# A three-block transformer kernel in float32: the order of the first loads, the memory's squares on GpSimd, and the third block's bias rows made in the second block

## The chip, the cores and the metric

The kernel runs on one core of a Trainium2 chip. The metric is the time of one launch on the device in microseconds (us), the median of several runs. The core has a matmul engine (TensorE, PE in the profile, with PEld for its weight loads), VectorE (DVE), ScalarE (ACT), GpSimd (POOL) and SyncE (SP), which only issues transfers. Each engine works through its own instructions in order. They wait for each other through semaphores, and transfers run on 16 DMA engines that SP and ACT feed through a queue each.

## The reference

256 tokens of 1024 numbers go through three blocks. Block 1 has two layers with a feed-forward part, three attention branches and a second feed-forward part. Block 2 has two layers (spatial gating, RWKV-7), block 3 one hybrid layer. The lines that the change is about:

```python
def first_block(x, mem, ...):
    mem_n = _rmsnorm(mem, mem_norm_g)            # 256 x 1024, used by both layers
    h = x
    for l in range(DEPTH):
        f = _swiglu(_rmsnorm(h, ffn1_pre_g[l]), ffn1_w_gate[l], ffn1_w_up[l], ffn1_w_down[l])
        h = h + 0.5 * _rmsnorm(f, ffn1_post_g[l])
        u = _rmsnorm(h, mix_pre_g[l])
        proj = u @ w_in[l]
        ...
        k_mem, v_mem = jnp.split(mem_n @ w_mem_kv[l], 2, axis=-1)
        ...

def nsa_attention(q, kc, vc, ks, vs, kw, vw, gates, tab):        # block 3, and moba_attention alike
        ...
        s_c = jnp.einsum('bthd,bnd->bhtn', qb, kc) + tab[:, rel_bucket(dist_c)][None]
```

`tab` is a table of 8 heads by 32 distance buckets. The kernel turns it into 8 "bias rows" of 512 distances, independent of x, and reads these as a banded matrix.

## The kernel before, in words

Everything that depends on x is a chain of matrix products in three passes: an operand is split into a high part (rounded for fast matmuls, made by ScalarE) and a low part (the rest, made by VectorE), and high x high, high x low and low x high are summed. The weights come as 440 **units** of 128 x 2048 numbers (1024 KB), always in the order of use. `sp_weights` (SP's queue) loads unit n into a ring of three slots, refilled when the low part of unit n - 3 is made. `hi` (ScalarE) makes its high part once unit n - 2 has been used up, `lo` (VectorE) the low part, and TensorE waits for the low part in `unit`. So the parts of a unit are made one unit ahead of their use. A unit of a feed-forward layer is 48 matmuls. Its units come as gate 0, up 0, gate 1, up 1, down 0, gate 2 and so on (`pe_ffn`, `act_ffn`, `dve_ffn`: `make` and `use`).

The order of each engine is that of the code. At the start (`sp_program`, `act_program`, `act_block1`):

- SP loads the constants (128 x 2432 numbers, 1216 KB, the identity first among them), x (1024 KB, into `h`), then the units.
- ScalarE loads the columns of gains (`pv`, 129 KB), waits for it and for the first unit, splits the first unit, and only then issues the loads of the norm rows (two rows, of which the first norm uses the second), of the forget weights (64 KB) and biases (8 KB) and of the memory (1024 KB). It waits for the forget weights, splits them, then does the first norm (`act_norm`).
- VectorE waits for constants and columns, makes the low part of the first unit, then of the forget weights, then norms x (`dve_norm`). TensorE turns the normed x (`pe_features`), ScalarE and VectorE split it (`act_features`, `dve_features`).
- Then, ahead of the first feed-forward layer, comes the norm of the memory: ScalarE squares it (`act_mean_sq`), TensorE sums the squares with a matrix of ones (`pe_mean_sq`, 8 matmuls), ScalarE takes the root (`act_std`), VectorE the reciprocal, and eight scalings (`dve_memory_norm`). The normed memory is read only after that feed-forward layer.

Between blocks all engines meet (`all_drained`). At the start of block 2 ScalarE issues three loads and then splits x. Its first feed-forward layer is followed by a norm, `pe_features` with 12 warming multiplies (`pe_warm`: products of the identity with itself, with no use but to keep TensorE busy) and the 16 units of the spatial gating (`sgu`). At the start of block 3 ScalarE splits x, then issues the loads of a one-hot matrix, a mask and the table; TensorE makes the bias rows from them (2 matmuls of 8 x 512 in bank 0), VectorE copies them out (`bias_rows`), ScalarE stores them in device memory (`bias_scratch`) and loads them back as a banded matrix (`bias_hankel`). The first projection of block 3 (`pe_project(k, pe, ("qn",), ...)`) stands behind the bias matmuls on TensorE, writes into bank 0, and so waits for the copy.

## Time and profile before

| | us |
|---|---|
| median of 3 runs | 3310.6 |
| lowest, highest | 3306.49, 3313.3 |
| profiled execution, its own time | 3313.89 |
| its span in the trace | 3312.1 |
| TensorE busy (matmuls) | 3056.4, 92% |
| VectorE, ScalarE, GpSimd busy | 1768.4, 1438.5, 177.9 |

The span is what the trace covers; 1.8 us of the execution's own time lie around it. TensorE is busy nearly throughout, so the chain of work that ended last is mostly its matmuls, and the rest of the chain are short stretches in which TensorE had nothing to do. Those stretches lie at the start of the kernel, around the norms, where the engines meet between blocks, and in the parts of blocks 2 and 3 that work step by step.

### The profile page before, as it was taken

What the parts mean: (1) busy time and instruction counts of PE and PEld (TensorE: products, weight loads), DVE (VectorE), ACT (ScalarE), POOL (GpSimd) and SP (SyncE); (2) the same over time, 40 slices, a digit from 0 to 9 for tenths busy, and PEclk for the clock granted to TensorE, in tenths of its full rate; (3) what the DMA queues carried; (4) which work ended last, traced back from release to release, by engine and by line L of the source; (5) the groups of instructions that cost most, each with busy time, mean ns of one, the idle gap of its engine ahead of it and who ended that gap; (6) DMA issues with size and microseconds to landing.
All of it is one profiled execution on the core that took longest, in us unless ns stands there. A gap on an engine that the chain in (4) does not pass through costs nothing.

```text
span 3312.1 us, 53914 instructions
## 1 busy us (share of the span) xinstructions
PE 3056.4 (92%) x23632; PEld 2817.4 (85%) x23632; DVE 1768.4 (53%) x2119; ACT 1438.5 (43%) x1822; POOL 177.9 (5%) x220
## 2 busy tenths in 40 slices
PE   6999899999999899999999999989799999685798
PEld 6998898999989889989898999978798988473787
DVE  4554555455555555455556555466755553435655
ACT  4454654444454554444454444444314442321344
POOL 0000100000000100010000000000200000703000
PEclk9999999999999999999999999989799997676899
DMA  5553344555543345555544555543103543110353
GB/s 210 189 185 109 127 140 166 186 183 179 190 153 141 115 141 178 190 208 187 204 170 160 180 189 178 188 144 140 40 5 132 187 178 128 63 39 13 115 178 140
DMA packets 69090, 492.73 MB, mean 149 GB/s; under 512 B 7933, under 2 KB 9373, under 8 KB 9846
## 3 DMA queue, kind: packets, MB, share of 16 engines
q1 hardware_dynamic: 63936, 464.74, 39.3%
q10 hardware_dynamic: 4922, 24.55, 2.0%
q8 instruction: 187, 3.06, 0.4%
q14 instruction: 45, 0.37, 0.0%
HBM read 488.17 MB, written 1.06 MB: 148 GB/s over the span
## 4 chain that ended last, share of the span: by engine, by line
PE 80%; DVE 9%; ACT 6%; issue 2%; POOL 1%; DMA 1%; PEld 0%; PEldq 0%; ACTq 0%; DVEq 0%; SPq 0%; POOLq 0%
PE bank L104 51%; PE acc L104 28%; DVE weights_lo L318 2%; ACT weights_hi L117 2%; DVE tmp L670 1%; DVE h L663 1%; POOL hgrn_pairs_q L3103 1%; DVE h L678 1%; PEld acc L104 0%; PE acc L992 0%; ACT b_x_hi L117 0%; ACT b_att_w_by_query L982 0%; ACT L1060 0%; DVE b_x_lo L502 0%; DMA weight_ring<-in_weights 0%
## 5 line engine op out<-in xcount | busy, mean ns | idle before, releaser
L318 DVE TENSOR_TENSOR weights_lo<-weight_ring,weights_hi 128x2048 fp32r<-128x2048 f32 x440 | 1009.6, 2295 | 993.8 <-ACT weights_hi L117 993.4
L104 PE MATMUL bank<-b_x_hi,weights_hi 128*128 128x256 f32 x3624 | 1025.3, 283 | 17.2 <-DVE b_x_lo L730 8.9
L104 PE MATMUL bank<-b_x_lo,weights_hi 128*128 128x256 f32 x3624 | 1020.3, 282 | 0.0
L104 PE MATMUL bank<-b_x_hi,weights_lo 128*128 128x256 f32 x3624 | 1019.5, 281 | 0.0
L117 ACT ACTIVATE weights_hi<-weight_ring 128x2048 fp32r<-128x2048 f32 x440 | 839.7, 1908 | 404.5 <-PE acc L104 372.2
L104 PEld LDWEIGHTS bank<-b_x_hi,weights_hi 128*128 128x128 f32 x3624 | 685.4, 189 | 32.4 <-issue 18.8
L104 PEld LDWEIGHTS bank<-b_x_lo,weights_hi 128*128 128x128 f32 x3624 | 684.8, 189 | 3.4
L104 PEld LDWEIGHTS bank<-b_x_hi,weights_lo 128*128 128x128 f32 x3624 | 685.3, 189 | 0.0
L104 PE MATMUL acc<-weights_hi,b_hidden_lo 128*128 128x512 f32 x832 | 328.2, 395 | 0.0
L104 PE MATMUL acc<-weights_hi,b_hidden_hi 128*128 128x512 f32 x832 | 328.1, 394 | 0.0
L104 PE MATMUL acc<-weights_lo,b_hidden_hi 128*128 128x512 f32 x832 | 328.0, 394 | 0.0
L117 ACT ACTIVATE b_hidden_hi<-act_gate 128x256 fp32r<-128x256 f32 x208 | 87.0, 418 | 341.8 <-DVE act_gate L883 313.0
L104 PEld LDWEIGHTS acc<-weights_hi,b_hidden_lo 128*128 128x128 f32 x832 | 156.2, 188 | 37.2
L861 ACT ACTIVATE act_gate<-bank 128x256 f32<-128x256 f32 x176 | 67.4, 385 | 276.3 <-PE bank L104 276.1
L104 PEld LDWEIGHTS acc<-weights_hi,b_hidden_hi 128*128 128x128 f32 x832 | 156.3, 188 | 33.6 <-DVE weights_lo L318 0.4
L104 PEld LDWEIGHTS acc<-weights_lo,b_hidden_hi 128*128 128x128 f32 x832 | 156.3, 188 | 33.1
L104 PE MATMUL bank<-weights_hi,b_x_hi 128*128 128x256 f32 (+2 forms) x544 | 156.4, 288 | 8.5 <-DVE weights_lo L318 8.2
L104 PE MATMUL bank<-weights_hi,b_x_lo 128*128 128x256 f32 (+2 forms) x544 | 156.1, 287 | 0.0
L104 PE MATMUL bank<-weights_lo,b_x_hi 128*128 128x256 f32 (+2 forms) x544 | 155.9, 287 | 0.0
L104 PE MATMUL acc<-b_x_hi,weights_hi 128*128 128x256 f32 x384 | 116.3, 303 | 14.0 <-ACT tmp L1060 8.8
L886 DVE TENSOR_TENSOR b_hidden_lo<-act_gate,b_hidden_hi 128x256 fp32r<-128x256 f32 x176 | 75.3, 428 | 85.3 <-ACT b_hidden_hi L117 85.3
L104 PEld LDWEIGHTS bank<-weights_hi,b_x_hi 128*128 128x128 f32 x544 | 107.8, 198 | 9.7 <-DVE weights_lo L318 9.1
(479 smaller groups left out, 4243.5 us busy)
## 6 DMA issues: line engine op xcount, KB each, us to landing
weight_ring<-in_weights SPq DMA_DIRECT2D x440, 1024.0 KB, 4.8
xn<-in_norm_rows ACTq DMA_DIRECT2D x15, 1024.0 KB, 4.8
sgu_bias_row<-in_sgu_rows ACTq DMA_DIRECT2D x1, 2048.0 KB, 9.2
sgu_norm_rows<-in_sgu_rows ACTq DMA_DIRECT2D x1, 2048.0 KB, 10.1
bias_hankel<-bias_scratch ACTq DMA_DIRECT2D x1, 1536.0 KB, 7.5
cons<-in_shape_constants SPq DMA_DIRECT2D x1, 1216.0 KB, 5.7
h<-in_x SPq DMA_DIRECT2D x1, 1024.0 KB, 7.8
mem_norm<-in_memory ACTq DMA_DIRECT2D x1, 1024.0 KB, 9.0
```

The lines of the kernel that those rows point to most:

```text
L104: return pe.matmul(out, a, b, start=start, stop=stop, skip_group_check=True)
L117: return act.activation(out, in_, ACT.Copy, scale=scale)
L318: dve.tensor_tensor(k.w.lo[:, n % 2, :], k.ring[:, n % RING, :], k.w.hi[:, n % 2, :], ALU.subtract) \
L663: dve.scalar_tensor_tensor(out=h, in0=h, scalar=alpha / scale, in1=acc_of(k, b), op0=ALU.mult, op1=ALU.add, accum_out=stat(k, 0, b)).then_ ...
L670: dve.scalar_tensor_tensor(out=k.t[:, b], in0=k.h[:, b, :], scalar=stat(k, 1, b), in1=k.rows[:, 0], op0=ALU.add, op1=ALU.mult).then_inc(*k ...
L678: dve.scalar_tensor_tensor(out=half(k.h[:, b], i), in0=half(k.t[:, b], i), scalar=stat(k, 6, b), in1=half(k.rows[:, 1], i), op0=ALU.mult, ...
L861: act.activation(k.act_gate[:, c, :], k.bank[c][:, 0:S], ACT.Silu).then_inc(*k.s.up("silu", f, j, c))
L886: dve.tensor_tensor(k.hid.lo[:, j % 2, c, :], k.act_gate[:, c, :], k.hid.hi[:, j % 2, c, :], ALU.subtract) \
L3103: pool.tensor_tensor(k.h_qp[0 if lag % 2 else 1][:, :, :], k.h_pr[:, :, :], k.h_q[:, :, :], ALU.mult) \
```

## The change

It has three parts.

1. **The first loads.** SP loads x in two halves with a semaphore each, units 0 and 1, the memory, unit 2, and the rest of the constants. ScalarE issues the identity alone, one norm row, the columns, then the forget weights and biases, none of them behind a wait for data, and loads the table of the root ahead of time. Its order is then: norm of x, high part of unit 0, split of x. The low part of unit 0 comes behind the norm on VectorE. TensorE runs 12 warming multiplies as soon as the identity is there. The split of the forget weights moves to the third and fourth step of the first feed-forward layer.
2. **The memory's norm.** GpSimd squares the memory (two products of 128 x 1024) and adds the halves (one sum of 128 x 1024). TensorE sums these with 4 matmuls, between up 0 and gate 1. ScalarE's root follows step 0, VectorE's reciprocal likewise, and the scalings stand four behind step 1 and four behind step 2.
3. **The bias rows.** Their three loads are issued at the start of block 2, behind the three loads that are there and ahead of the split of x. The two matmuls (bank 1) stand ahead of the turn of x before the spatial gating, with 2 warming multiplies in place of 12. The copy stands behind the split of that x on VectorE, the store behind it on ScalarE. At the start of block 3 the load of the banded matrix remains.

```diff
-def sp_weights(k, sp):
+def sp_weights(k, sp, between={}):
     for n in range(len(k.plan)):
+        if n in between:
+            between[n]()
         if n >= RING:
...
-    act.dma_start(k.rows, bass.AP(tensor=k.aps["norm_rows"].tensor, offset=at, ap=[[0, P], [1, 2 * D]])) \
+    n = 1 if of == ("pre1", 0) else 2
+    act.dma_start(k.rows[:, 2 - n:], bass.AP(tensor=k.aps["norm_rows"].tensor, offset=at, ap=[[0, P], [1, n * D]])) \
...
+def pool_memory(k, pool):
+
+    pool.wait_ge(*k.s.at("loaded_mem"))
+    for i in range(2):
+        pool.tensor_tensor(k.mem_sq[:, 4 * i:4 * i + 4, :], k.memn[:, 4 * i:4 * i + 4, :],
+                           k.memn[:, 4 * i:4 * i + 4, :], ALU.mult).then_inc(*k.s.up("mem_sq", i))
+    pool.wait_ge(*k.s.at("mem_sq", 1))
+    pool.tensor_tensor(k.mem_sq[:, 0:4, :], k.mem_sq[:, 0:4, :], k.mem_sq[:, 4:8, :], ALU.add) \
+        .then_inc(*k.s.up("mem_sum"))
+
+
+def pe_memory(k, pe):
+    pe.wait_ge(*k.s.at("loaded_cons"))
+    out = empty(k, pe, 4, ("std", ("memory",)))[:, 0:S]
+    pe.wait_ge(*k.s.at("mem_sum"))
+    for j in range(4):
+        i = mm(pe, out, k.con("ones"), k.mem_sq[:, j, :], j == 0, j == 3)
+    i.then_inc(*k.s.up("mean_sq", ("memory",)))
...
-    pe_features(k, pe, ("pre1", l), k.t, in_parts(("pre1", l)), warm=12 * l,
+    pe_features(k, pe, ("pre1", l), k.t, in_parts(("pre1", l)), warm=12,
                 midway=("made", ("ffn2", 0), 1, 0) if l else None)
-    if l == 0:
-        pe_mean_sq(k, pe, ("memory",), KT, k.mem_sq)
-    pe_ffn(k, pe, ("ffn1", l), *ffn_units(1, l), split_mark(("pre1", l)))
+    pe_ffn(k, pe, ("ffn1", l), *ffn_units(1, l), split_mark(("pre1", l)), {} if l else {0: lambda: pe_memory(k, pe)})
...
-    act_ffn(k, act, ("ffn1", l))
+    act_ffn(k, act, ("ffn1", l), {} if l else {0: lambda: act_memory(k, act), 2: lambda: act_forget_weights(k, act)})
...
+    dve_ffn(k, dve, ("ffn1", l), {} if l else {
+        0: lambda: dve_rstd(k, dve, ("memory",)), 1: lambda: dve_memory(k, dve, range(0, 4)),
+        2: lambda: dve_memory(k, dve, range(4, 8)), 3: lambda: dve_forget_weights(k, dve)})
...
 def act_program(k, act):
+    act.dma_start(k.cons[:, 0:P], k.aps["shape_constants"][:, 0:P]).then_inc(*k.s.landed("loaded_ident"))
+    act_load_rows(k, act, ("pre1", 0))
     act.dma_start(k.pv[:, :], k.aps["columns"]).then_inc(*k.s.landed("loaded_pv"))
-    act.wait_ge(*k.s.at("loaded_pv"))
+    act.preload_act_table(ACT.Sqrt)
     act.wait_ge(*k.s.at("eps_set"))
-    hi(k, act)
...
-    sp.dma_start(k.cons[:, :], k.aps["shape_constants"]).then_inc(*k.s.landed("loaded_cons"))
-    sp.dma_start(k.h[:, :, :], k.aps["x"]).then_inc(*k.s.landed("loaded_x"))
-    sp_weights(k, sp)
+    for b in range(NB):
+        sp.dma_start(k.h[:, b, :], k.aps["x"][:, b, :]).then_inc(*k.s.landed(f"loaded_x{b}"))
+    sp_weights(k, sp, {2: lambda: sp.dma_start(k.memn[:, :, :], k.aps["memory"]).then_inc(*k.s.landed("loaded_mem")),
+                       3: lambda: sp.dma_start(k.cons[:, P:], k.aps["shape_constants"][:, P:])
+                       .then_inc(*k.s.landed("loaded_cons"))})
```

The bias rows' part (the same statements leave `pe_attention3`, `act_attention3` and `dve_attention3`):

```diff
+def act_bias_loads(k, act):
+    for n, x, name in (("hot", k.hot, "bias_one_hot"), ("mrow", k.mrow, "bias_mask"), ("tabT", k.tabT, "bias_table")):
+        act.dma_start(x[:, :], k.aps[name]).then_inc(*k.s.landed(f"loaded_{n}"))
...
     pe_ffn(k, pe, ("f2", 0, 0), *ffn2_units(0, 0), split_mark(("in2",)))
-    pe_features(k, pe, ("r2", 0, 0), k.h, in_parts(("r2", 0, 0)), warm=12)
+    pe_bias_rows(k, pe)
+    pe_features(k, pe, ("r2", 0, 0), k.h, in_parts(("r2", 0, 0)), warm=2)
     pe_sgu(k, pe)
...
+    act_bias_loads(k, act)
     act_features(k, act, ("in2",))
...
     act_next2(k, act, ("r2", 0, 0), 0.5, ("r2", 0, 1))
+    act_bias_store(k, act)
     act_sgu(k, act)
...
     dve_next2(k, dve, ("r2", 0, 0), 0.5, ("f2", 0, 0))
+    dve_bias_rows(k, dve)
     dve_sgu(k, dve)
```

How the instructions of the program stand in a row, at three places. First ScalarE at the start of the kernel (`pv` are the columns, `cons` the constants, `xn` holds the norm rows, `q` the squares of the memory). Before:

```order
L3464 DMA pv<-in_columns 128x258
L117 ACT_TABLE_LOAD [waits s_w_raw0,s_gpsimd_pads]
L117 ACTIVATE weights_hi<-weight_ring 128x2048 [waits s_loaded_pv]
L573 DMA xn<-in_norm_rows 128x2048
L1493 DMA w_forget<-in_w_forget 128x128
L1494 DMA b_forget<-in_b_forget_rows 128x16
L1495 DMA mem_norm<-in_memory 128x2048
L117 ACTIVATE w_forget_hi<-w_forget 128x128 [waits s_loaded_wf]
L627 ACTIVATE act_gate,norm_stats<-h 128x1024 [waits s_loaded_x]
```

And with the change:

```order
L3530 DMA cons<-in_shape_constants 128x128
L576 DMA xn<-in_norm_rows 128x1024
L3532 DMA pv<-in_columns 128x258
L3533 ACT_TABLE_LOAD
L1546 DMA w_forget<-in_w_forget 128x128 [waits s_gpsimd_pads]
L1547 DMA b_forget<-in_b_forget_rows 128x16
L630 ACTIVATE act_gate,norm_stats<-h 128x1024 [waits s_loaded_x0]
L632 ACTIVATE norm_stats<-norm_stats,epsc 128x1 [waits s_sq_sum]
L630 ACTIVATE act_gate,norm_stats<-h 128x1024 [waits s_loaded_x1]
L632 ACTIVATE norm_stats<-norm_stats,epsc 128x1 [waits s_sq_sum]
L118 ACTIVATE weights_hi<-weight_ring 128x2048 [waits s_w_raw0]
```

All loads now stand ahead of the first wait for data, and the high part of unit 0 stands behind the norm of x instead of ahead of it.

Second, ScalarE in the first feed-forward layer, from the high part of up 0 on. Before:

```order
L117 ACTIVATE weights_hi<-weight_ring 128x2048 [waits s_w_raw1]
L861 ACT_TABLE_LOAD
L861 ACTIVATE act_gate<-bank 128x256 [waits s_gate] x2
L117 ACTIVATE weights_hi<-weight_ring 128x2048 [waits s_gate,s_w_raw2]
L117 ACTIVATE b_hidden_hi<-act_gate 128x256 [waits s_glu] x2
L117 ACTIVATE weights_hi<-weight_ring 128x2048 [waits s_upper,s_w_raw0]
L861 ACTIVATE act_gate<-bank 128x256 [waits s_hid_lo,s_gate] x2
```

And with the change:

```order
L118 ACTIVATE weights_hi<-weight_ring 128x2048 [waits s_w_raw1]
L866 ACT_TABLE_LOAD
L866 ACTIVATE act_gate<-bank 128x256 [waits s_gate] x2
L118 ACTIVATE weights_hi<-weight_ring 128x2048 [waits s_gate,s_w_raw2]
L118 ACTIVATE b_hidden_hi<-act_gate 128x256 [waits s_glu] x2
L1287 ACT_TABLE_LOAD
L1287 ACTIVATE rstd<-acc,epsc 128x256 [waits s_mean_sq]
L118 ACTIVATE weights_hi<-weight_ring 128x2048 [waits s_upper,s_w_raw0]
L866 ACT_TABLE_LOAD [waits s_hid_lo]
L866 ACTIVATE act_gate<-bank 128x256 [waits s_gate]
```

A table load and the memory's root now stand ahead of the high part of up 1 (unit 3), and a second table load behind it.

Third, ScalarE at the start of block 2, with the change (before, the rows with L1661 are not there, and stand as L2869 behind the split of x at the start of block 3):

```order
L2594 DMA sgu_w_spatial<-in_sgu_w_spatial 128x2048 [waits s_end_pool,s_end_dve,s_end_pe]
L2595 DMA sgu_b_spatial<-in_sgu_b_spatial 128x16
L2597 DMA sgu_bias_row<-in_sgu_rows 128x4096
L1661 DMA bias_one_hot<-in_bias_one_hot 32x512
L1661 DMA bias_mask<-in_bias_mask 1x512
L1661 DMA bias_table<-in_bias_table 32x8
L118 ACTIVATE b_x_hi<-bank 128x512 [waits s_turned_h] x2
L118 ACTIVATE b_x_hi<-acc 128x512 [waits s_turned_h] x2
```

The three loads of the bias rows now stand between the meeting of the engines and the split of x.

## Rows read from the trace of the kernel before

**Rows 1.** The page: the span, and the chain that ended last by engine.

```profile
span 3312.1 us, 53914 instructions
...
PE 80%; DVE 9%; ACT 6%; issue 2%; POOL 1%; DMA 1%; PEld 0%; PEldq 0%; ACTq 0%; DVEq 0%; SPq 0%; POOLq 0%
```

**Rows 2.** The chain, 0 to 60 us: start, duration in us, what.

```profile
11.97 7.23 DMA w_forget<-in_w_forget
...
41.82 17.23 PE bank L104 x144
```

**Rows 3.** Timeline of the opening: start, duration in us, engine, line, instruction [idle before].

```profile
1.18 0.42 SPq L3495 DMA_DIRECT2D h<-in_x  x1
...
19.43 1.04 ACT L627 ACTIVATE act_gate<-h 128x1024 f32<-128x1024 f32 x1
...
20.58 1.28 ACT L629 ACT_TABLE_LOAD   x1
21.88 0.29 ACT L629 ACTIVATE norm_stats<-norm_stats,epsc 128x1 f32<-128x1 f32 x1
...
25.81 1.09 ACT L117 ACTIVATE b_x_hi<-bank 128x512 fp32r<-128x512 f32 x2 [2.27 <-PE bank L708]
...
28.44 5.54 PE L104 MATMUL bank<-q,cons 128*128 128x256 f32 x16 [1.39 <-ACT q L520]
...
34.52 1.75 DVE L540 RECIPROCAL rstd<-rstd 128x256 f32<-128x256 f32 x1 [5.60 <-ACT rstd L535]
...
36.31 3.26 DVE L548 SCALAR_TENSOR_TENSOR mem_norm<-mem_norm,pv,rstd 128x256 f32<-128x256 f32 x8
...
41.82 0.39 PE L104 MATMUL bank<-b_x_hi,weights_hi 128*128 128x256 f32 x1 [1.19 <-DVE weights_lo L318]
...
48.56 1.90 ACT L117 ACTIVATE weights_hi<-weight_ring 128x2048 fp32r<-128x2048 f32 x1
...
50.49 2.29 DVE L318 TENSOR_TENSOR weights_lo<-weight_ring,weights_hi 128x2048 fp32r<-128x2048 f32 x1 [1.38 <-ACT weights_hi L117]
```

**Rows 4.** Timeline at the start of block 2: the split of x on ScalarE.

```profile
1456.65 0.60 ACT L117 ACTIVATE b_x_hi<-bank 128x512 fp32r<-128x512 f32 x1 [4.70 <-issue]
```

**Rows 5.** Timeline at the start of block 3.

```profile
2732.05 0.45 ACTq L2869 DMA_DIRECT2D bias_one_hot<-in_bias_one_hot  x1
...
2732.86 0.32 ACTq L2869 DMA_DIRECT2D bias_table<-in_bias_table  x1
...
2733.60 1.28 DVE L730 TENSOR_TENSOR b_x_lo<-acc,b_x_hi 128x512 fp32r<-128x512 f32 x2
...
2740.79 0.68 DVE L2944 COPY bias_rows<-bank 8x512 f32<-8x512 f32 x1 [5.91 <-PE bank L104]
...
2741.57 0.55 PE L104 MATMUL bank<-b_x_hi,weights_hi 128*128 128x256 f32 x1 [0.82 <-issue]
```

**Rows 6.** Windows, 0 to 10 us: busy per engine, granted clock, DMA share, GB/s.

```profile
0.00:5.00 5.00, 0.00 (x0) 0.00 (x0) 0.00 (x0) 0.00 (x0) 0.47 (x10) 1.00 0.66 221
5.00:10.00 5.00, 0.00 (x0) 0.00 (x0) 0.00 (x0) 0.00 (x0) 0.00 (x0) 1.00 1.01 425
```

**Rows 7.** Transfers of the opening: size, and us from issue to landing.

```profile
h<-in_x SPq DMA_DIRECT2D x1, 1024.0 KB, 7.8
```

**Rows 8.** Windows, in the first unit of block 2 (PE busy first, then PEld, DVE, ACT, POOL).

```profile
1459.00:1462.00 3.00, 3.00 (x16) 3.00 (x15) 2.32 (x3) 2.80 (x2) 0.00 (x0) 0.50 0.98 407
```

**Rows 9.** Groups by form on GpSimd: busy us, mean ns, idle before.

```profile
L3103 POOL TENSOR_TENSOR hgrn_pairs_q<-hgrn_pairs,hgrn_q 128x512 f32<-128x512 f32 x15 | 19.4, 1292 | 38.0 <-DVE hgrn_pairs L3080 38.0
```

**Rows 10.** One tile, the spatial weights masked on GpSimd: ns minimum/median/maximum.

```profile
L1762 POOL TENSOR_TENSOR sgu_w_spatial<-sgu_w_spatial,cons x16: 455/464/2505, 1465.5 to 1474.3; 128x128 f32<-128x128 f32 x16
```

**Rows 11.** Timeline of VectorE beside the last of those.

```profile
1474.33 2.55 DVE L318 TENSOR_TENSOR weights_lo<-weight_ring,weights_hi 128x2048 fp32r<-128x2048 f32 x1 [1.18 <-ACT weights_hi L117]
```

**Rows 12.** Timeline at the start of the spatial gating in block 2.

```profile
1655.41 0.55 PE L104 MATMUL bank<-weights_hi,b_x_hi 128*128 128x256 f32 x1 [0.22 <-DVE b_x_lo L730]
...
1655.78 1.28 DVE L730 TENSOR_TENSOR b_x_lo<-acc,b_x_hi 128x512 fp32r<-128x512 f32 x2
```

105 lines of the change are left out of this document (57 added, 48 removed).

## Prediction

> **What bounds the kernel now.** I read the page first. The chain that ended last is TensorE for 80% [rows 1], so nearly all of the span is matmuls that the change leaves alone, and what can move is time in which TensorE stands still. I looked for that in three places that the diff touches, in order of time.
>
> The opening. The chain [rows 2] shows 7.23 us of waiting for the forget weights: ScalarE issued their load only at 11.97, behind its first weight split, and everything queued on ScalarE stood behind it. The squares of x start at 19.43, with a table load of 1.28 in their chain; the split x leaves at 25.81; then come the memory's squares and their 16 matmul records (28.44 to 33.98), 0.54 to the reciprocal, which takes 1.75, and eight scalings of 3.26 [rows 3]. The second unit of the first feed-forward layer (up 0) starts at 41.82, after TensorE had waited 1.19 for its low part. That is the place from which I count.
>
> Block 2's start: ScalarE splits x at 1456.65, directly behind three DMA issues [rows 4]. Block 3's start: x is ready at 2733.60 + 1.28 = 2734.88, but the first projection starts at 2741.57, since the bias rows are copied out of bank 0 until 2740.79 + 0.68 = 2741.47 [rows 5].
>
> **The change part by part.**
>
> *Loads.* The windows [rows 6] give 221 GB/s over the first 5 us (1.10 MB) and 425 after. x in the kernel before is behind the constants: 1216 + 1024 KB, with the columns' 129 KB beside them, 2.43 MB, passed at 5 + 1.33/0.425 = 8.1; it landed at 1.18 + 7.8 = 9.0 [rows 3, 7], so a signal comes 0.9 behind its bytes. In the change the first weight unit has 2825 KB up to and with it (x 1024, norm row 512, identity 64, columns 129, forget weights and biases 72, itself 1024), 2.89 MB: 5 + 1.79/0.425 + 0.9 = 10.1. x's two halves, with the norm row beside them, land before 7.5 by the same sum.
>
> *The path to the first matmul.* ScalarE's norm work starts with x, by 7.5 at the latest, and from its start to the split of x it took 25.81 - 19.43 = 6.4 before, 5.1 without the table load, now preloaded. That gives 11 to 12.6. The weights are as late: the first high part 10.1 to 12.0 (1.90 each, [rows 3]), low part to 14.3 (2.29), then one of two low parts of x (1.28 for two, [rows 5]): the first matmul at 15.0. The uncertain step is the landing: 0.7 either way.
>
> *Gate 0 and the clock.* 144 matmuls took 17.23 [rows 2], 0.12 each, so a unit of 48 takes 5.75. TensorE idles ahead of the first one, which before followed the memory's matmuls closely. A stretch at the lower level stands in [rows 8], after block 2's idle start: at granted 0.50 (1.2 GHz) 16 matmuls in 3 us, where the upper level (2.4 GHz) does 25; a loss of 1.1. The twelve warming multiplies at the start speak for no loss, the same twelve ahead of block 2 did not save it from that stretch. Ends 0 and 1.8; I take 1.4. Gate 0 ends at 22.2 and up 0 at 27.95. The low part of up 0 follows the fourth low part of x (16.9 + 2.3 = 19.2), so up 0 no longer stalls.
>
> *The memory's mean square.* Eight matmuls become four (8 records; the sum over the other half is GpSimd's). The 16 records took 5.54 at mixed clocks: 1.9 at 0.12 per 256 columns and pass, 2.8 by the mean. I take 1.9, as TensorE is then at the upper level. Gate 1 starts at 29.85. Before it started at 41.82 + 5.75 = 47.57. **The opening gains 17.7.**
>
> That holds if these are covered. GpSimd: the trace has no 1024-wide product; 512 wide takes 1.29 [rows 9], so 2.4 to 2.6 each if no fixed part helps, three from the memory's landing (4.99 MB: 15.0): done at 22.8, 5 ahead of need. ScalarE: between the hidden activations and the third unit's high part it now has a table load (1.28) and the root; the order is in front of this text. Before, high part 3 started 1.0 after up 0 ended, and its low part ended at 52.78, 0.5 before gate 1 did. Now: 28.95, table to 30.2, root to 30.65 (0.54 less the hand-over), high part to 32.55, low part to 34.9, gate 1 ends at 35.6: still 0.7 early, because the four matmuls push the need back. The reciprocal (1.75) fits beside the high part. The eight scalings (half of 3.26 twice) and the forget split stand behind low parts with over 2 us of room.
>
> The Trainium skill, ScalarE: Activation LUTs, section "What ACT_TABLE_LOAD costs", adds a drain of about 1.4 us to each load. The table row starts at 20.58, lasts 1.28, and the root starts at 21.88 [rows 3]: no such drain. By the page the low part would end near 36.3 and the sum lose 0.7.
>
> *Sharing between VectorE and GpSimd.* A mask product of usually 0.46 took up to 2.5 [rows 10], and the low part beside the last of them, at 1474.33, took 2.55 instead of 2.29 [rows 11]: the two hold each other up. Here low part 1, ready at 16.9, meets the first or second GpSimd product. At worst it waits for the rest of both: 15.0 + 2 x 2.5 = 20.0, done 22.3, needed at 22.2. So 0 to 0.1; with products half as slow again, 2.6. I take 0, since it would more likely get in behind the first product. The Trainium skill, SBUF — State Buffer, section "SBUF: two separate sides", says that the pair of ports is locked for a whole instruction; the trace agrees by the 2.5 us.
>
> *Block 2's start.* Three more DMA issues stand before the split of x. At block 3 the same three run from 2732.05 to 2733.18 [rows 5]: **a loss of 1.15**. TensorE's idle time ahead of it grows by as much; its clock there already falls for 3 us or more [rows 8], and I price a longer stretch at 0 to 1.8 and take 0.
>
> *Bias rows in block 2.* Four matmul records of 512 columns take the place of ten warming multiplies, while TensorE waits for the norm: at 0.24 for 512 columns and pass some 1.9 in place of 2.4 at the same rate, hidden. VectorE's copy (0.68, [rows 5]) comes after the last x_lo (1655.78 + 1.28 = 1657.06, [rows 12]); ScalarE's store waits for it, and the second unit's high part stands behind that store in ScalarE's queue: 1658.1 to 1660.0, low part to 1662.3. TensorE started the first unit at 1655.41 and at the slower clock for part of it needs the second at 1661.9 to 1662.9. So a loss of 0 to 0.4; if narrow matmuls (32 rows) do not keep the clock up, 1.2 more. I take 0.
>
> *Block 3's start.* No load, matmul, copy or store is waited for: the first projection starts at 2735.0 and not at 2741.57, **a gain of 6.6**. It starts at the lower clock in both. The store was long ago, the hankel load is issued some 10 us earlier.
>
> **Sum.** 17.7 + 6.6 - 1.15 = 23.1. Against the profiled execution, 3313.9 (span 3312.1 and 1.8 around it): 3290.8. That execution lies 3.3 above the median 3310.6, so the median of the change should be 3287.5; I say 3288.
>
> **The rivals.**
>
> *A, the opening gives less.* The weight unit lands later, since two queues share the engines from the start, or the GpSimd products and the low part collide, or root and table load miss their 0.7 us. Each costs 1 to 2; together 3 to 6 of the 17.7: 3291 to 3294. For it: the sharing in [rows 10, 11]. Against it: each has some cover.
>
> *B, the gain is larger.* The clock stays up in the opening (1.4) and transfers run faster early: 3284 to 3286. For it: the warming multiplies run from the identity's landing; against it: the slow stretch at block 2 [rows 8].
>
> *C, the gain is real and is absorbed.* If a later stage ran by something that keeps its own time (the weight stream), both stalls would come back as waits there: 3311. Against it: the weight ring is refilled when VectorE has read a slot, nothing in the chain waits for it after the opening, and TensorE is 80% of it.
>
> *D, slower.* TensorE now waits for GpSimd in the middle of the first layer, and gate 1 with all its followers waits behind. It is slower than before once the memory's sum comes later than 27.95 + 23.1 = 51, which would take products of 12 us each. At 15 us each: 3320. The widest row of 512 elements speaks against it. That the change does not do what it says would be seen as gate 1 still near 47, 3304 with block 3's part alone.
>
> **How the numbers follow.** The forecast 0.60, A 0.22, B 0.12, C (and the change's opening failing) 0.04, D 0.02. A measurement of this kernel tells 0.2% (6.6 us) from no change. Faster by more: 0.95; within: 0.03; slower: 0.02. The range takes the forecast's own costs (clock 0 to 1.8 twice, landing 0.7), B, most of A and the spread of the runs before (3306.5 to 3313.3): 3281 to 3295.
>
> **What would show it.** Opening: first product of the feed-forward layer at 15.0, gate 1 at 29.85, GpSimd done by 23, no TensorE wait on the memory's sum. Block 2: ScalarE's split 1.15 later behind the drained engines, and SGU's second unit without a wait. Block 3: from last x_lo to first projection 0.1 instead of 6.7. The prediction is wrong if the first product comes after 18, if TensorE waits for GpSimd, or if the low part of unit 1 or 3 is late.

## The result and the profile after

The change takes 3288.73 us (median of five runs, 3285.31 to 3295.76) where the kernel before takes 3310.6 (five runs, 3306.49 to 3317.3): a ratio of 0.9939, 95% interval 0.9926 to 0.9951, that is 20.2 us of 3310.6, and 16.2 to 24.5 by the interval. The forecast was a time of 3288, from a sum of 23.1. The profiled execution took 3288.73, its span 3286.9, and is 25.2 shorter than the profiled one of before. So the interval puts the forecast sum inside, near its upper part, and the single pair of traces shows more than the median does. Where these three numbers part is told below.

The page of the change, span and chain by engine, beside [rows 1]:

```profile
span 3286.9 us, 53907 instructions
...
PE 80%; DVE 9%; ACT 6%; issue 2%; POOL 1%; PEld 0%; DMA 0%; PEldq 0%; ACTq 0%; DVEq 0%; SPq 0%; POOLq 0%
```

The chain of the change, 0 to 60 us, beside [rows 2] (start, duration in us, what):

```profile
1.65 9.35 DMA weight_ring<-in_weights
...
11.02 1.92 ACT weights_hi L118
...
12.97 2.29 DVE weights_lo L319
15.26 0.61 DVE b_x_lo L733
...
16.01 13.04 PE bank L105 x96
29.04 1.73 PE acc L105 x8
30.77 11.31 PE bank L105 x96
42.08 5.60 PE acc L105 x24
```

From 16.01 on the chain is TensorE alone. The forget weights, which ScalarE waited 7.23 us for, are gone from it; what is first now is the landing of the first weight unit. The 13.04 us are gate 0 and up 0 (96 records), 1.73 the memory's matmuls, and gate 1 starts at 30.77. The first down projection starts at 42.08, where before it started at 41.82 + 17.23 = 59.05 [rows 2].

The windows of both traces between four marks give the account of the 25.2 us: the first down projection, the first load of the spatial gating unit (issued when block 2 begins), the first split of x in block 3, and block 3's first projection. Columns: window, length, busy us with instructions for PE, PEld, DVE, ACT, POOL, granted clock, DMA share, GB/s. First the kernel before, then the change.

```profile
59.05:1455.30 1396.25, 1333.20 (x9860) 1259.51 (x9859) 738.62 (x863) 689.59 (x884) 43.94 (x80) 0.98 0.46 162
1455.30:2731.67 1276.37, 1215.25 (x10772) 1133.66 (x10772) 719.16 (x805) 532.53 (x620) 35.00 (x34) 0.96 0.43 155
2731.67:2741.57 9.90, 3.57 (x5) 0.41 (x5) 3.16 (x5) 2.06 (x4) 0.21 (x2) 0.50 0.36 126
2741.57:3312.10 570.53, 472.03 (x2772) 393.34 (x2772) 283.03 (x416) 190.97 (x284) 98.25 (x94) 0.81 0.27 96
```

```profile
42.08:1437.13 1395.05, 1331.03 (x9860) 1257.81 (x9859) 741.72 (x872) 689.89 (x885) 43.90 (x80) 0.99 0.45 162
1437.13:2713.20 1276.07, 1213.61 (x10756) 1129.87 (x10756) 719.05 (x806) 531.74 (x620) 34.96 (x34) 0.96 0.43 155
2713.20:2716.76 3.56, 0.00 (x0) 0.03 (x1) 2.48 (x4) 3.56 (x5) 0.21 (x2) 0.50 0.70 255
2716.76:3286.90 570.14, 471.91 (x2772) 393.17 (x2772) 283.14 (x416) 189.16 (x284) 98.13 (x94) 0.81 0.27 96
```

Opening 59.05 - 42.08 = 16.97; block 1 from there 1.20; block 2 0.30; block 3's start 9.90 - 3.56 = 6.34; the rest 0.39. Sum 25.2. Block 2 holds the added issues and yet shows a small gain, so something else in it went the other way. It is one place. Between the starts of the 349th and the 350th low part of the weights the kernel before takes 11.59 us, with 5 us of it at granted 0.50, and the change 8.46 at granted 1.00, for the same stretch of the program (windows of the kernel before, then of the change; a count takes in what overlaps an edge):

```profile
2310.72:2322.31 11.59, 10.39 (x67) 9.87 (x67) 5.64 (x8) 5.29 (x8) 0.00 (x0) 0.79 0.24 90
2296.42:2304.88 8.46, 7.26 (x62) 7.03 (x61) 5.64 (x9) 5.30 (x8) 0.00 (x0) 1.00 0.32 124
```

Ten of the twelve traces other than that of the kernel before have 8.43 to 8.46 here, and two have 10.0. So 3.1 of the 25.2 us belong to that one execution of the kernel before, and not to the change. In block 1 the same 9860 matmuls took 2.2 us less of TensorE's busy time.

The start of block 2 and that of block 3 in the change (timeline), beside [rows 4] and [rows 5]:

```profile
1438.46 0.45 ACTq L1661 DMA_DIRECT2D bias_one_hot<-in_bias_one_hot  x1
1438.94 0.30 ACTq L1661 DMA_DIRECT2D bias_mask<-in_bias_mask  x1
1439.27 0.32 ACTq L1661 DMA_DIRECT2D bias_table<-in_bias_table  x1
1439.64 0.60 ACT L118 ACTIVATE b_x_hi<-bank 128x512 fp32r<-128x512 f32 x1 [5.87 <-issue]
...
1441.20 0.55 PE L105 MATMUL bank<-b_x_hi,weights_hi 128*128 128x256 f32 x1 [4.16 <-DVE b_x_lo L733]
```

```profile
2715.13 1.28 DVE L733 TENSOR_TENSOR b_x_lo<-acc,b_x_hi 128x512 fp32r<-128x512 f32 x2
...
2716.76 0.55 PE L105 MATMUL bank<-b_x_hi,weights_hi 128*128 128x256 f32 x1 [3.65 <-DVE b_x_lo L733]
```

The split waits 5.87 for issues where it waited 4.70, 1.17 more. In block 3 the first projection stands 0.35 behind the last low part of x (2715.13 + 1.28 = 2716.41), where it stood 6.7 behind it.

### The profile page after: what moved, and what is told of

Same layout as the page of the kernel before. It is cut to its first block, busy times and chain, and to the rows that moved or that the text cites. A ratio compares the mean times of both kernels' runs of the same rounds, so it can differ in the third digit from the quotient of the medians.

```text
span 3286.9 us, 53907 instructions
## 1 busy us (share of the span) xinstructions
PE 3049.4 (93%) x23628; PEld 2813.3 (86%) x23628; DVE 1767.6 (54%) x2119; ACT 1436.7 (44%) x1819; POOL 185.9 (6%) x223
## 4 chain that ended last, share of the span: by engine, by line
PE 80%; DVE 9%; ACT 6%; issue 2%; POOL 1%; PEld 0%; DMA 0%; PEldq 0%; ACTq 0%; DVEq 0%; SPq 0%; POOLq 0%
PE bank L105 51%; PE acc L105 28%; DVE weights_lo L319 2%; ACT weights_hi L118 2%; DVE tmp L673 1%; DVE h L666 1%; DVE h L681 1%; POOL hgrn_pairs_q L3169 1%; PEld acc L105 0%; PE acc L1001 0%; DVE b_x_lo L505 0%; DVE b_x_lo L733 0%; ACT b_att_w_by_query L991 0%; ACT L1069 0%; ACT L1135 0%
## 5 line engine op out<-in xcount | busy, mean ns | idle before, releaser
L105 PE MATMUL bank<-b_x_hi,weights_hi 128*128 128x256 f32 x3624 | 1027.7, 284 | 22.5 <-DVE b_x_lo L733 17.1
L105 PEld LDWEIGHTS bank<-b_x_hi,weights_hi 128*128 128x128 f32 x3624 | 687.4, 190 | 35.8 <-issue 20.2
## 6 DMA issues: line engine op xcount, KB each, us to landing
cons<-in_shape_constants SPq DMA_DIRECT2D x1, 1152.0 KB, 19.8
```

Source lines behind the costliest of these rows:

```text
L105: return pe.matmul(out, a, b, start=start, stop=stop, skip_group_check=True)
```

## The experiments

Eleven kernels ran. Their ratios are to the kernel before, timed on the same chip beside them. A ratio is estimated from all runs of both kernels, so it need not be that of the two medians. The intervals reach 3.5 to 5 us to each side; what is smaller than that is read from traces, and a trace is one execution.

**The third part alone, and the change without it.** Edit of the first (the second is the change with the same lines taken back):

```diff
 def pe_block2(k, pe):
...
-    pe_features(k, pe, ("r2", 0, 0), k.h, in_parts(("r2", 0, 0)), warm=12)
+    pe_bias_rows(k, pe)
+    pe_features(k, pe, ("r2", 0, 0), k.h, in_parts(("r2", 0, 0)), warm=2)
...
 def act_block2(k, act):
...
+    act_bias_loads(k, act)
     act_features(k, act, ("in2",))
...
+    act_bias_store(k, act)
     act_sgu(k, act)
```

> The kernel before with the third part of the change alone (bias loads, matmuls, copy and store in block 2). The theory, from the trace of the change: block 3's first projection starts 6.3 us earlier than it did, three issues of 1.15 us stand before the split at block 2's start, and TensorE's stretch at the lower level there is 6.8 us long instead of 3.4, which costs another 1.5. Net gain 3 to 4 us: a ratio of 0.9988 to 0.9991 to the kernel before. Rival one, the prediction's own terms (6.6 less 1.15, clock at nothing): 5.4 us, 0.9984. Rival two: block 2's loss eats the gain, 0 to 1 us. In the profile: last low part of x to first projection of block 3 under 0.5 us, where it was 6.7.

> The change without its third part: bias rows loaded, made, copied and stored at block 3's start as before. The theory: the opening brings 17 us at the start of the first down projection and nothing is given back, so 16 to 19 us under the kernel before (ratio 0.9943 to 0.9952) and 3 to 5 above the change. Rival: the third part nets nothing, and this kernel equals the change (0.9939). Block 2's start then has three DMA issues again, and the stretch at the lower level there is 3.4 us again.

Measured: 0.9987 (0.9976 to 0.9997; 3312.14 beside 3314.22) and 0.9949 (0.9937 to 0.9962; 3297.43). 4.3 us for the third part, 16.9 for the rest, 21.2 in sum; the change has 20.2. They add up, and each is near what the trace of the change shows at its place: 17.0 at the opening; 6.34 less 1.17 less 1.2 of clock (next) less 0.6 at the gating unit (below) = 3.4 for the third part. The interval of the first, 1.0 to 8.0 us, doesn't part 3.4 from the prediction's 5.4, and its two medians lie only 2.1 apart; the terms are the traces'. Block 3's start in the first kernel, last low part to first projection 2730.59 + 1.28 to 2732.23, is 0.36.

The trace of the first kernel also shows a stall of TensorE at the second unit of the spatial gating, the place that the prediction priced at 0 to 0.4 and took at 0. ScalarE's second weight split waits 2.07 us for the copy of the bias rows, as in the change, whose row stands first; TensorE's wait in this kernel stands second:

```profile
1642.16 1.92 ACT L118 ACTIVATE weights_hi<-weight_ring 128x2048 fp32r<-128x2048 f32 x1 [2.07 <-DVE bias_rows L1671]
```

```profile
1662.85 0.39 PE L104 MATMUL bank<-weights_hi,b_x_hi 128*128 128x256 f32 x1 [0.46 <-DVE weights_lo L318]
```

Three more traces with the copy there have such a wait (0.35 to 0.53 us, among them that of the change once more). In the change's first trace none is listed, since TensorE ran at the lower level for part of its first unit, but the second unit starts at the same distance: 1646.53 - 1639.49 = 7.04 us behind the first, and 1662.85 - 1655.81 = 7.04 here. In the kernel before it was 1661.85 - 1655.41 = 6.44, and in the change without its third part, which has no copy there either, 7.6, with more of the unit at the lower level. So the copy in front of the store sets a floor of 7.04, and its price hangs on the clock: 0.6 us against the trace of the kernel before, nothing in that other kernel.

**The bias loads behind the split.**

```diff
-    act_bias_loads(k, act)
     act_features(k, act, ("in2",))
     act_load_rows(k, act, ("r2", 0, 0))
+    act_bias_loads(k, act)
```

> The change with the three bias loads issued behind the split of x and the row load in block 2. The theory: ScalarE's split starts 1.15 us earlier against the end of block 1, and the stretch at the lower level there is 3.4 us again and not 6.8: 1.2 to 2.7 us faster than the change. Rival: the lower level's length has nothing to do with these issues, 1.15 us only. Second rival: ScalarE's first weight split behind them is now late by 1.1 us and its low part with it, so that the second unit waits and the gain is nothing.

Measured: 0.9932 (0.992 to 0.9945), 2 us under the change and within what runs stray. The trace tells it: the split waits 4.71 for issues again, and this is what TensorE does in the 7 us from its first product in block 2 (PE first), in the kernel before, in the change, and in this kernel:

```profile
1458.22:1465.22 7.00, 7.00 (x46) 7.00 (x47) 3.94 (x4) 3.58 (x4) 0.00 (x0) 0.76 1.01 424
```

```profile
1441.20:1448.20 7.00, 7.00 (x36) 7.00 (x37) 3.94 (x4) 3.58 (x4) 0.00 (x0) 0.56 0.99 389
```

```profile
1443.41:1450.41 7.00, 7.00 (x46) 7.00 (x47) 3.94 (x4) 3.58 (x4) 0.00 (x0) 0.76 1.00 421
```

46 matmuls, 36, and 46 again. Ten matmuls are 1.2 us at 0.12 each. So in this pair of traces the three issues cost 1.17 us twice over: once as the wait, and again because TensorE, waiting 4.16 us for the first product and not 3.00, stays at granted 0.50 (1.2 GHz) for longer. The other traces give the sign but not one size. In all with three issues ahead of the split TensorE waits 3.00 us and does 46 or 47 matmuls (three traces, that of the change without its third part among them). In the eight with six issues it waits 4.16 to 4.35 us and does 36, 36, 36, 36, 37, 40, 41 and 43. The second cost is 0.4 to 1.2 us, most often 1.2.

**Multiplies that keep TensorE busy, first ahead of the drain, then behind it.** In the first kernel (fill) they stand between and behind the transposes at four starts; in the second 14 stand behind the point where all engines have waited for each other, at block 2 alone:

```diff
                 if q % 2:
                     a.then_inc(*k.s.up("turned_h", of, b, p))
+        pe_warm(k, pe, fill[b], 0)
...
-    pe_features(k, pe, ("in2",), k.h, in_parts(("in2",)), warm=12, made=("ffn2", 1))
+    pe_features(k, pe, ("in2",), k.h, in_parts(("in2",)), warm=12, made=("ffn2", 1), fill=(2, 12))
```

```diff
 def pe_block2(k, pe):
     k.x, k.hid = k.x2, k.hid2
+    pe_warm(k, pe, 14, 0)
```

> The change with more identity multiplies on TensorE between and behind the transposes at four starts: 12 behind at the opening, 2 between and 12 behind at block 2's start, 4 between and 8 behind at the spatial gating unit and at block 3. The theory: TensorE's idle time of 3 to 4 us ahead of the first product is what the granted clock falls after, and filled, the stretches at 17.1, 1440.5 and 1635.1 are gone or shorter: each 3.4 us at granted 0.50 costs 1.5 to 1.7, so 3 to 8 us faster than the change. Rival: the clock falls all the same, as at block 2 with its twelve multiplies ahead of the transposes, and 12 multiplies take 2.8 us at the upper and 5.1 at the lower level, so that the first products start up to 1 us later: 0 to 3 us slower.

> The change with 14 identity multiplies on TensorE at block 2's start, behind the wait of all engines for each other. In the earlier kernel with such multiplies they stood ahead of the drain, and ScalarE's loads and split started 2.8 us later by it. The theory: here they take 3.3 us at the upper level and end before the first product, which waits 4.1 us for the split of x; the start of block 2 is not delayed, and the stretch at the lower level of 6.8 us is gone: 3 us faster than the change. Rival: the clock falls all the same, since the idle times ahead of the transposes have already happened, and nothing is gained; the multiplies at the lower level take 5.9 us and delay the first product by 1.8.

Measured: 0.9942 (0.9928 to 0.9955) and 0.9932 (0.9919 to 0.9944). The first is no faster than the change, and its trace says why. This is TensorE at block 2's start in it:

```profile
1438.79 0.66 PE L711 MATMUL bank<-cons,h 128*128 128x128 f32 x4
1439.45 0.66 PE L711 MATMUL acc<-cons,h 128*128 128x128 f32 x4
1439.94 2.84 PE L105 MATMUL bank<-cons 128*128 128x128 f32 x24
...
1447.14 0.55 PE L105 MATMUL bank<-b_x_hi,weights_hi 128*128 128x256 f32 x1 [4.35 <-DVE b_x_lo L734]
```

The twelve multiplies (24 records) run for 2.84 us ahead of TensorE's drain, ScalarE's issues wait for that drain, and the wait ahead of the first product is still 4.35 us, with 36 matmuls in the 7 us behind it. Cover put ahead of a point at which all engines meet delays them all. Neither theory had this. Block 3's start in the same kernel shows it too: eight multiplies (16 records, 1.95 us) ahead of the drain, and still a wait of 3.63 us for the first product, 3.65 in the change. At the opening, where no engine waits for TensorE's drain, the twelve left a wait of 0.96 us and no slow stretch (59 matmuls in 7 us). Behind that point it works: 28 records from 1438.41, TensorE waits 0.65, and the 7 us from the first product hold 59 matmuls at full clock:

```profile
1442.42:1449.42 7.00, 7.00 (x59) 7.00 (x60) 3.94 (x4) 4.97 (x7) 0.62 (x2) 1.00 1.01 406
```

23 more than the change's 36, 2.7 us at 0.12, and 16 more, 1.9 us, than the 43 of the change run once more. The timed median, 3289.22 beside 3291.84 for the change in the same session, agrees with it, but these two don't part by themselves.

**The order beside the units.** The memory's mean square, root, reciprocal and scalings go ahead of the first unit on all three engines, as before; loads and GpSimd's squares stay as in the change.

```diff
+    if l == 0:
+        pe_memory(k, pe)
-    pe_ffn(k, pe, ("ffn1", l), *ffn_units(1, l), split_mark(("pre1", l)), {} if l else {0: lambda: pe_memory(k, pe)})
+    pe_ffn(k, pe, ("ffn1", l), *ffn_units(1, l), split_mark(("pre1", l)))
...
+    if l == 0:
+        act_memory(k, act)
...
+    if l == 0:
+        dve_rstd(k, dve, ("memory",))
+        dve_memory(k, dve, range(8))
```

> The change with the memory's mean square, root, reciprocal and all eight scalings ahead of the first feed-forward unit on TensorE, ScalarE and VectorE, as the order was before; loads and GpSimd's squares as in the change. It tells what the order beside the units is worth, apart from the loads. The theory: TensorE waits until GpSimd's sum at 24.6, its four matmuls end at 26.4, gate 0 ends at 32.2; reciprocal and scalings end at 32.7 and the low part of up 0 at 35.0, so gate 1 starts at 40.8 where the change has 30.77: 10 us slower than the change, and still 7 faster than before. Rival: GpSimd's work is not what counts and its end comes earlier without a low part beside it; gate 1 at 37 or less, 6 us slower.

Measured: 0.9961 (0.9947 to 0.9976), some 7 us behind the change. The first down projection starts at 52.67, 10.6 later than in the change (10 expected; 1.5 of it for the constants, below). Of the opening's 17 us, then, 10.6 are the order beside the units, and 6.4 all that this kernel keeps: the loads, the forget weights' place, the table loaded ahead and GpSimd's sum. No run parts these 6.4 us further, but for the 1.7 of the sum (below). Something not expected stands in its chain:

```profile
4.01 20.01 DMA cons<-in_shape_constants
...
24.07 3.54 PE acc L105 x8
...
35.44 17.23 PE bank L105 x144
```

TensorE waits for the rest of the constants, not for GpSimd, whose sum was done at 20.13 + 2.34 = 22.5. In the change they land at the same time, 19.8 us after their issue at 4.18, and the memory's matmuls start at 29.04: 5 us of cover that the prediction did not count, since it had looked at GpSimd alone.

**GpSimd's products twice.**

```diff
     pool.wait_ge(*k.s.at("mem_sq", 1))
+    for i in range(2):
+        pool.tensor_tensor(k.mem_sq[:, 4 * i:4 * i + 4, :], k.memn[:, 4 * i:4 * i + 4, :],
+                           k.memn[:, 4 * i:4 * i + 4, :], ALU.mult).then_inc(*k.s.up("mem_sq", 2 + i))
+    pool.wait_ge(*k.s.at("mem_sq", 3))
```

> The change with each of GpSimd's two products of the memory made twice; results are the same. It measures the cover of the wait that the change puts into TensorE's queue. The theory: products of 2.9 us each beside VectorE, so the sum ends near 24.6 + 5.8 = 30.4, and the memory's matmuls, which started at 29.04, wait for it: gate 1 starts at 32.2 instead of 30.77, and what stands behind it, the root, the third high and low parts, moves with it; loss 1.4 to 3 us at the start of the first down projection. Rival: the prediction's cover (5 us) holds or GpSimd is faster without a low part beside it (2.4 each): the sum by 29.4, loss under 0.5 us.

Measured: 0.9936 (0.9923 to 0.9949). The timing can't tell it from the change; the chain can:

```profile
16.27 5.81 POOL q L1269 x2
...
22.14 5.81 POOL q L1273 x2
...
28.02 2.41 POOL q L1276
...
30.57 1.96 PE acc L105 x8
32.53 10.89 PE bank L105 x96
```

The sum ends at 30.43 as expected, TensorE waits 3.5 us for it, and gate 1 starts at 32.53. The first theory holds: the first down projection starts at 43.42, 1.3 behind the change's, where 1.4 to 3 was expected. With its products once, GpSimd is done at 24.6, and TensorE would have asked at 27.1 here: in an opening at full clock the cover is 2.5 to 3 us, in the change's own trace 4.4, and the prediction said 5.

**The squares on ScalarE.** They are made after the second weight split, in ScalarE's wait for gate 0, and all eight parts are summed by TensorE:

```diff
     def make(j):
         hi(k, act)
+        if j == 0 and beside:
+            act_memory_squares(k, act)
...
-    for j in range(4):
+    for j in range(8):
```

> The change with the memory's squares by ScalarE, between the second weight split and the first hidden activation, in which it waits for gate 0, and no sum of the halves: eight matmuls (16 records) instead of four. GpSimd does nothing there. The theory: ScalarE's squares (2 x 1.06) and table load end by 20.3, before gate 0 does; the low part of the second unit takes 2.29 instead of 2.79; TensorE loses only the four matmuls, 1.73 us: gate 1 starts 1.7 later than in the change, a loss of 1 to 2 us. Rival: taking the work off ScalarE is what the opening's gain comes from, and with it back there a stall of 3 us or more shows at gate 0 or up 0.

Measured: 0.9938 (0.9925 to 0.9951), the change's ratio. Gate 1 starts at 30.63, where 1.7 later than the change's 30.77 was expected: the slow stretch behind the first product is missing in this trace, and against the kernel with late bias loads, where it is missing too (gate 1 at 29.22), it is 1.4 later. ScalarE does both squares in 2.03 us from 16.59, table load done at 19.9; no stall anywhere; the memory's matmuls take 3.45 instead of 1.73. So what GpSimd gives is 1.7 us of TensorE's time, by the sum of the halves; that the squares are off ScalarE gives nothing, once they stand beside a unit. One tile tells of sharing: GpSimd's two products of equal size (minimum, median, maximum in ns), first in the change, then in the kernel with the memory ahead, where VectorE makes no weight part beside them:

```profile
L1269 POOL TENSOR_TENSOR q<-mem_norm x2: 1893/2917/3941, 16.3 to 18.2; 128x1024 f32<-128x1024 f32 x2
```

```profile
L1269 POOL TENSOR_TENSOR q<-mem_norm x2: 1891/1892/1892, 16.3 to 18.2; 128x1024 f32<-128x1024 f32 x2
```

1.89 without it, 3.94 beside the second low part of the weights, and that low part takes 2.79 in the change and 2.28 in the kernel with ScalarE's squares, without GpSimd:

```profile
17.57 2.79 DVE L319 TENSOR_TENSOR weights_lo<-weight_ring,weights_hi 128x2048 fp32r<-128x2048 f32 x1
```

```profile
17.61 2.28 DVE L318 TENSOR_TENSOR weights_lo<-weight_ring,weights_hi 128x2048 fp32r<-128x2048 f32 x1
```

VectorE loses 0.5 us, the rest of the first product that was running when it started, and GpSimd's second product 2.05. In the kernel with the products made twice the fourth product meets a low part again: it takes 3.945, and the low part, which started first at 23.85, takes 2.33 and loses nothing to speak of. So the one that comes second pays. The Trainium skill, SBUF — State Buffer, section "SBUF: two separate sides", has the pair of ports locked for a whole instruction; the second product's 2.05 us on top, close to a whole low part, agree with it.

**Fewer bytes ahead of the first weight unit.**

```diff
 def act_program(k, act):
-    act.dma_start(k.pv[:, :], k.aps["columns"]).then_inc(*k.s.landed("loaded_pv"))
...
 def act_block1(k, act):
-    act.dma_start(k.wf[:, :], k.aps["w_forget"]).then_inc(*k.s.landed("loaded_wf"))
-    act.dma_start(k.bf[:, :], k.aps["b_forget_rows"]).then_inc(*k.s.landed("loaded_bf"))
...
 def sp_program(k, sp):
...
+        sp.dma_start(k.memn[:, :, :], k.aps["memory"]).then_inc(*k.s.landed("loaded_mem"))
+        sp.dma_start(k.pv[:, :], k.aps["columns"]).then_inc(*k.s.landed("loaded_pv"))
+        sp.dma_start(k.wf[:, :], k.aps["w_forget"]).then_inc(*k.s.landed("loaded_wf"))
+        sp.dma_start(k.bf[:, :], k.aps["b_forget_rows"]).then_inc(*k.s.landed("loaded_bf"))
```

> The change with the columns and the forget weights and biases loaded from SyncE's queue behind the memory instead of from ScalarE's beside x (201 KB less ahead of the first weight unit). The theory: the landing of the first weight unit at 11.0 follows the bytes ahead of it: 0.20 MB less at 0.424 MB per us brings it to 10.5, and the first product from 16.0 to 15.5: 0.5 us at the start of gate 1, too little for the timed runs to tell. Rival: the landing is set by the issues and by the small rows of these loads, 10.0 or less and a gain of 1 us or more; or VectorE's work sets the first product and it stays at 16.0.

Measured: 0.9931 (0.9916 to 0.9946). The unit lands at 10.56 instead of 11.0, the first product stands at 15.57 instead of 16.01: 0.44 for 0.20 MB at 0.424 MB per us (0.47), as the theory had it.

**The change once more.**

> The change itself once more, unaltered, as the measure for the two beside it and for how far a second execution's trace strays. The theory: TensorE's stretches at the lower level differ from one execution to the next by several us in sum, also ahead of gate 0, where they are there in some executions and not in others after the same idle time; ratio to the kernel before 0.993 to 0.995, as before. The part of the trace without TensorE idle times agrees with the first within 0.2 us. Rival: the stretch behind the first product (3.4 us in the first trace of the change) belongs to it and is there again.

Measured: 0.994 (0.9927 to 0.9954). Same program, same opening (first down projection at 41.95, the change's 42.08), and then the windows between the marks of the account:

```profile
41.95:1434.09 1392.14, 1326.73 (x9860) 1253.16 (x9859) 741.38 (x872) 690.01 (x885) 43.97 (x80) 0.99 0.45 162
1434.09:2711.51 1277.42, 1214.93 (x10756) 1130.81 (x10756) 720.40 (x806) 531.70 (x619) 34.95 (x34) 0.96 0.43 155
...
2715.07:3290.40 575.33, 476.77 (x2772) 394.74 (x2772) 283.17 (x416) 189.30 (x284) 98.27 (x94) 0.81 0.26 95
```

Block 1 is 2.9 us shorter than in the change's first trace and the last part 5.2 longer, and TensorE's busy time differs by as much (4.3 and 4.9), for equal numbers of matmuls; VectorE, ScalarE and GpSimd agree within 0.4 in both windows. So a single window differs by up to 5 us from one execution of the same program to the next, and it is TensorE's pace that differs. Part of that is the granted clock: in the 40 us from 262 TensorE got 236 matmuls through at granted 0.91 in the first trace and 261 at 1.00 in the second. Part of it is not. Here are eighteen weight units of block 2 in which TensorE never stands still, in the first trace and in the second:

```profile
1874.17:1975.97 101.80, 101.80 (x723) 95.48 (x722) 50.59 (x42) 42.81 (x42) 0.00 (x0) 1.00 0.52 187
1872.77:1975.37 102.60, 102.60 (x723) 96.22 (x722) 50.92 (x42) 42.81 (x42) 0.00 (x0) 1.00 0.51 185
```

The same 723 matmuls, both at granted 1.00, and 0.8 us between them. So the expectation that stretches without idle time agree within 0.2 us failed, and the cause of this second part is open. The stretch behind the first product was there again. It is not there in every execution of this opening: in the 5 us from 16.0 TensorE got 30 matmuls through in the change and 43 in the kernel with late bias loads, whose opening is the same:

```profile
16.00:21.00 5.00, 4.99 (x30) 5.00 (x31) 4.36 (x4) 1.96 (x2) 4.68 (x2) 0.66 1.02 425
```

```profile
16.00:21.00 5.00, 5.00 (x43) 5.00 (x44) 4.33 (x4) 1.91 (x2) 4.71 (x2) 1.00 1.02 425
```

It was there in four of the nine traces in which this opening is unfilled and the first product follows (TensorE waited 3.35, 3.64, 3.64 and 2.93 us for it) and not in five (3.10, 2.73, 2.59, 2.55, 2.32). The longer waits have it, but 2.93 with and 3.10 without overlap, so the wait alone doesn't decide.

**A version to beat the change.**

```diff
 def act_block2(k, act):
-    act.dma_start(k.wsp[:, :, :], k.aps["sgu_w_spatial"]).then_inc(*k.s.landed("loaded_wsp"))
...
-    act_bias_loads(k, act)
     act_features(k, act, ("in2",))
...
-    act_ffn(k, act, ("f2", 0, 0))
...
+    act_ffn(k, act, ("f2", 0, 0), {0: lambda: act_sgu_loads(k, act, rows), 1: lambda: act_bias_loads(k, act)})
...
-    act_bias_store(k, act)
     act_sgu(k, act)
...
         for b in range(NB):
             act_sgu_tile(k, act, 2 * i + b)
+        if i == 1:
+            act_bias_store(k, act)
...
 def pe_block3(k, pe):
-    for j in range(0, KT, 2):
-        pe.wait_ge(*k.s.at(*split_mark(("in3",))(j)))
-    pe_project(k, pe, ("qn",), [w3(Q_N)], took_both(("qn",)))
+    pe_project(k, pe, ("qn",), [w3(Q_N)], took_both(("qn",)), split_mark(("in3",)))
```

with the small loads behind the memory as above.

> A version meant to beat the change. Block 2: the spatial gating unit's three loads are issued behind ScalarE's work on the first unit and the three bias loads behind the second, none ahead of the split of x; the store of the bias rows stands behind the second of the gating unit's column groups; block 3's first projection starts with the first low part of x and doesn't wait for the fourth; columns and forget weights load behind the memory. The theory: six issues of 2.5 us in sum leave the path at block 2's start, and with them 1.5 us of the lower level; at block 3 the first product starts 1.9 us earlier against the split; the first weight unit brings 0.4: 5 to 6.5 us under the change, ratio 0.9915 to 0.993 to the kernel before. Rival: the issues hold up a weight split that is needed by then, or the starts fall to the lower level and give it back; then 0 to 2 us.

Measured: 3285.88 beside 3311.03, 0.992 (0.9906 to 0.9933), against 0.994 for the change in the same session: some 6 us faster, as expected (5 to 6.5), though the two intervals overlap. It is four edits at once, and no run parts them. Its block 2 start, the window behind it, and its block 3 start:

```profile
1437.28 0.60 ACT L118 ACTIVATE b_x_hi<-bank 128x512 fp32r<-128x512 f32 x1 [3.35 <-PEq L341]
...
1438.85 0.36 PE L105 MATMUL bank<-b_x_hi,weights_hi 128*128 128x256 f32 x1 [1.65 <-DVE b_x_lo L733]
```

```profile
1438.85:1445.85 7.00, 7.00 (x59) 7.00 (x60) 3.93 (x4) 4.97 (x7) 0.00 (x0) 1.00 0.48 184
```

```profile
2711.13 0.55 PE L105 MATMUL bank<-b_x_hi,weights_hi 128*128 128x256 f32 x1 [1.65 <-DVE b_x_lo L733]
```

With no issue ahead of the split TensorE waits 1.65 us and not 4.16, and stays at the upper level by itself, 59 matmuls in 7 us. Block 3's first projection starts 1.57 behind the first split (2709.56) where it stood 3.56 behind. The issues do cost 0.5 us elsewhere: TensorE waits that long for the low part behind the gating unit's loads. With the store moved, ScalarE's second weight split of the gating no longer waits for the copy; its low part starts 2.50 us behind the first product (1637.67 - 1635.17) and not 4.69.

## Why the prediction was right

The sign, the places and the size were right; two small steps at block 2 were not. The steps one by one:

- *Loads.* The first weight unit was to land at 10.1 and landed at 11.0. The part that was off is the first 5 us: I took the 221 GB/s of the kernel before [rows 6], and the window 0 to 5 of the change has 158, 0.79 MB instead of 1.10. With 0.79 the same sum gives 5 + 2.10/0.424 + 0.9 = 10.85. The small-loads kernel, whose landing moved by 0.44 for the 0.47 of its bytes, bears out the rest of that sum.
- *First product.* 15.0 forecast, 16.01 measured; 0.9 of it from the landing. The two low parts and the high part took what the rows said.
- *Gate 0 and the clock.* The price of 1.4 for a stretch at the lower level was right where the stretch appears (13.04 in the change against 11.54 in the kernel with late bias loads, 1.5), but it is not in every execution.
- *The memory's mean square.* 1.9 forecast, 1.73 measured. Gate 1 stood at 30.77, not 29.85.
- *The cover.* GpSimd was done at 24.6, not 22.8: the memory landed at 16.2 instead of 15.0, and the collision with VectorE cost it 2.05. The low part of unit 3 ended at 33.66 + 2.29 = 35.95, before gate 1's end at 36.4: 0.5 early, where 0.7 was forecast, and TensorE does not wait between 16.01 and 60. The table load in front of the memory's root starts at 29.98, lasts 1.28, and the root starts at 31.28, so the drain of some 1.4 us that the Trainium skill (ScalarE: Activation LUTs, "What ACT_TABLE_LOAD costs") adds did not show here either. What I had not counted, the constants, had 5 us.
- *Block 2's start.* 1.15 forecast for the issues, 1.17 measured. I took nothing out of 0 to 1.8 for a longer stretch of the clock, and the kernel with late bias loads shows that it was 1.2 in the change's trace (0.4 to 1.2 over all). This is the term that was mis-sized most. I had the mechanism, and had noted that the idle time grew, and still took the lower end.
- *The gating unit.* ScalarE's second weight split waited 2.07 us for the copy of the bias rows, as feared, and its low part ended 6.98 us behind the first product, where 6.9 was forecast. What was off is the need: TensorE asked for the second unit at 6.44 us in the kernel before, and not between 6.5 and 7.5. That cost 0.6 against that trace, where I took 0 out of 0 to 0.4, and by my own sign, "SGU's second unit without a wait", this step failed in four traces.
- *Block 3's start.* 6.6 forecast, 6.34 measured.

In sum 17.0 + 6.34 - 1.17 - 1.2 - 0.6 = 20.4 by the places, where the forecast had 23.1. The timed runs say 20.2, and 19.9 for the change run once more (by its 0.994 of 3311.03), the two parts timed apart 21.2. Of the remaining 4.8 us of the 25.2 between the two profiled traces, 3.1 are the slow stretch of the kernel before at 2310.72, and the rest lies within what one execution differs from the next. So the forecast came out within 1 us of the median partly by luck: the sum was 2.7 us too large, and the median of the first five runs, 3288.73, is a little below what its own ratio gives (0.9939 of 3310.6 is 3290.4). Rival A, an opening that gives less, was right in kind (the unit landed later, the products collided) but only by 0.7 us.

## What to carry to other kernels

A wait taken out of a start can be worth more than its length: here 1.17 us of DMA issues ahead of a split cost 0.4 to 1.2 more, because TensorE then ran at the lower level for longer. Issue loads behind the first work of a stage when they are needed later, and put filler work behind the point where engines meet: ahead of it, it delayed the others at both places tried here. When one trace of each kernel differs by more than the account of the edited places, run one of them again before explaining the rest: here a repeated execution strayed by up to 5 us in one window. And compare the starts of work that both kernels do alike, the low parts of the weights here: that shows at which instruction two traces part.

## What the runs showed of the hardware

- TensorE at block 2's start, matmuls in the 7 us from its first product: idle 1.65 us or filled but for 0.65, none of it at 0.50, 59; idle 3.00, 46 or 47 (three traces); idle 4.16 to 4.35, 36 to 43 (eight traces).
- The same 723 matmuls took 101.80 and 102.60 us in two executions of one program, both at granted 1.00 and without an idle time.
- A GpSimd product of 128x1024 takes 1.89 us, and 3.94 when a low part on VectorE stands beside it; I had estimated 2.4 to 2.6 from the 512-wide one [rows 9]. The sum of two such tiles took 2.34 with nothing beside it, near the estimate; whether it is the same tile read twice or the product that makes the squares cheaper was not tried.
- The transfers of the first 5 us moved 158 GB/s in the change and 221 before, and 425 in both afterwards. Which of the new order's loads slows the start was not tried.
